# Dilated attention: value projections of 384 columns over a pair's three groups, and four weight units a pair

## The reference

```python
def mixer_dilated(x, w_in, w_out, table):
    proj = x @ w_in                       # [256, 1024] @ [1024, 3 * 3 * 1024]
    gw = 3 * ATTN_WIDTH
    for g, (window, dilation) in enumerate(DILATED_PAIRS):
        q, k, v = [split_heads(t, N_HEADS) for t in jnp.split(proj[..., g * gw:(g + 1) * gw], 3, axis=-1)]
        o, lse = dilated_group(q, k, v, table, window, dilation)
        outs.append(o); lses.append(lse)
    wts = jax.nn.softmax(jnp.stack(lses), axis=0)
    o = jnp.einsum('gbhs,gbhsd->bhsd', wts, jnp.stack(outs).astype(jnp.float32))
    return merge_heads(o.astype(x.dtype)) @ w_out
```

## Time and profile before

| what | value |
|---|---|
| median of 3 runs | 2671.15 us (2669.37 to 2674.56) |
| profiled execution | 2666.07 us, span of its instructions 2664.1 us, mean granted TensorE clock 0.962 |
| busy over the span | PE 2478.7 us (93%), weight loads 2106.7 us (79%), DVE 1533.5 us (58%), ACT 1098.9 us (41%), POOL 20.5 us (1%) |
| 896 products of 256 columns, high x high, in the page | 292 ns each, 261.6 us |
| 608 products of 512 columns, high x high, feed-forward | 393 ns each, 239.1 us |
| 24 loads of dilated weights | 1536 KB each, 6.7 us from issue to landing (median) |

### The profile page before, as it was taken

How to read it: one execution, slowest core, us unless ns; L and a number is a source line. 1 busy time by engine, 2 the same in 40 slices (tenths; PEclk the granted TensorE clock), 3 DMA queues, 4 the chain that set the end, 5 groups by cost and what they waited for, 6 DMA issues and landing times.

```text
span 2664.1 us, 37436 instructions
## 1 busy us (share of the span) xinstructions
PE 2478.7 (93%) x15464; PEld 2106.7 (79%) x15464; DVE 1533.5 (58%) x2133; ACT 1098.9 (41%) x1150; POOL 20.5 (1%) x35
## 2 busy tenths in 40 slices
PE   7999999999999799998999978889999999896997
PEld 6999986888879578886887956768878888484886
DVE  3334334666668646667666456466656654754565
ACT  3333332455446425554554322145545533312553
POOL 1000000000000000000000000000000000000000
PEclk9999988999999879999999989989999999999999
DMA  5333323355522315554454411025535543100453
GB/s 206 113 137 107 133 111 111 135 187 185 186 112 96 134 57 189 188 186 170 151 186 183 158 48 71 2 98 187 188 140 189 189 159 141 60 12 33 144 187 110
DMA packets 35712, 358.29 MB, mean 134 GB/s; under 512 B 4111, under 2 KB 4255, under 8 KB 6544
## 3 DMA queue, kind: packets, MB, share of 16 engines
q1 hardware_dynamic: 32512, 342.39, 35.3%
q0 software_dynamic: 3104, 14.51, 1.7%
HBM read 355.76 MB, written 1.12 MB: 134 GB/s over the span
## 4 chain that ended last, share of the span: by engine, by line
PE 83%; DVE 9%; ACT 4%; DVEq 2%; issue 1%; DMA 1%; ACTq 0%; SPq 0%
PE psum L663 21%; PE psum L412 12%; PE psum L413 11%; PE psum L414 11%; PE psum L665 10%; PE psum L614 2%; PE psum L1800 2%; DVE ring_lo L426 1%; PE psum L943 1%; PE psum L1811 1%; PE psum L921 1%; PE psum L1807 1%; ACT ring_hi L420 1%; PE psum L788 1%; PE psum L552 1%
## 5 line engine op out<-in xcount | busy, mean ns | idle before, releaser
L663 PE MATMUL psum<-xT_both,ring_hi 128*128 128x512 f32 x2432 | 874.4, 402 | 2.3 <-DVE ring_lo L426 2.2
L426 DVE TENSOR_TENSOR ring_lo<-ring,ring_hi 128x3072 fp32r<-128x3072 f32 (+1 forms) x188 | 622.7, 3312 | 245.7 <-ACT ring_hi L420 245.7
L665 PE MATMUL psum<-xT_both,ring_lo 128*128 128x256 f32 x2432 | 685.7, 282 | 0.0
L663 PEld LDWEIGHTS psum<-xT_both,ring_hi 128*128 128x128 f32 x2432 | 461.4, 190 | 119.0 <-DVE ring_lo L426 4.8
L420 ACT CAST ring_hi<-ring 128x3072 fp32r<-128x3072 f32 (+1 forms) x188 | 511.1, 2719 | 43.7 <-DMA ring<-moe_w 29.6
L665 PEld LDWEIGHTS psum<-xT_both,ring_lo 128*128 128x128 f32 x2432 | 463.3, 190 | 5.8
L706 ACT COPY scratch<-psum 128x512 f32<-128x512 f32 x152 | 89.4, 588 | 607.2 <-PE psum L665 607.2
L412 PE MATMUL psum<-xT_both,ring_hi 128*128 128x256 f32 x896 | 261.6, 292 | 23.6 <-DVE ring_lo L1027 11.0
L413 PE MATMUL psum<-xT_both,ring_hi 128*128 128x256 f32 x896 | 256.6, 286 | 0.0
L414 PE MATMUL psum<-xT_both,ring_lo 128*128 128x256 f32 x896 | 256.3, 286 | 0.0
L412 PE MATMUL psum<-ring_hi,glu_hi 128*128 128x512 f32 x608 | 239.1, 393 | 3.2 <-DVE glu_lo L743 3.2
(11 more groups left out here) (356 smaller groups left out, 3257.8 us busy)
## 6 DMA issues: line engine op xcount, KB each, us to landing
ring<-ff_w SPq DMA_DIRECT2D x88, 1536.0 KB, 6.6
ring<-moe_w SPq DMA_DIRECT2D x64, 1536.0 KB, 6.6
ring<-dil_w SPq DMA_DIRECT2D x24, 1536.0 KB, 6.7
ring<-mix_w SPq DMA_DIRECT2D x20, 1536.0 KB, 6.7
ring<-proj_w SPq DMA_DIRECT2D x16, 1024.0 KB, 4.8
ring<-sb_w SPq DMA_DIRECT2D x8, 1536.0 KB, 6.7
scratch<-rel_dram POOLq DMA_DIRECT2D x16, 384.0 KB, 4.4
rowv<-row_vectors POOLq DMA_DIRECT2D x4, 1024.0 KB, 5.0
```

The source lines that it names most:

```text
L426: nc.vector.tensor_tensor(ring_lo[:, s, 0:floats], ring[:, s, 0:floats], ring_hi[:, s, 0:floats].bitcast(F32), ALU.subtract).then_inc(low_ ...
L663: nc.tensor.matmul(psum[:, bank, :].rearrange("p (w n) -> p w n", w=2), ring_hi[:, s, cols], xT_both[:, :, k, :], start=(k == 0), stop=False)
L665: last = nc.tensor.matmul(psum[:, bank, 0:SEQ], ring_lo[:, s, cols], xT_hi[:, k, :], start=False, stop=(k == KC - 1))
```

## The change

The weights of the dilated stage are laid out anew: per pair three units with Q and K of one group (2048 floats a partition, 1 MB) and one unit with V of all three groups (3072 floats, 1.5 MB), in slots 0 to 2 and 3. `ring_hi` gets a second view, `dil_hi`, in which the four units stand one behind the other. `project_v(p, t)` now makes one tile of tokens for all three groups at once: 24 products of 384 moving columns, twice a pair, and `take_v` copies 384 columns. SP loads in the order 0, V, 1, 2, and asks for a slot again when PE has read it (`qk_ready`, `v_ready`), not when the copy is done. PE's order in a pair becomes scores 0, 1, QK 0, turn 0, scores 2, V of tile 0, weigh 0, turn 1, V of tile 1, scores 3, weigh 1, turn 2, QK 1, weigh 2, turn 3, QK 2, weigh 3. The lists of DVE and ACT, and what all three do ahead of the loop, are changed with it. The counts of `high_ready` and `low_ready` go up by four a pair.

```diff
     out = {"x": f["x"][0], "rel_table": f["rel_table"], "router_b": f["router_b"],
            "router_w": rows(f["router_w"]), "positions": f["positions_2"].astype(np.int32)}
     w = f["dil_w_in"][0].reshape(KC, P, GROUPS, 3, PAIRS, P)
-    out["dil_w"] = w.transpose(4, 2, 1, 0, 3, 5).reshape(PAIRS, GROUPS, P, UNIT)
+    out["dil_qk"] = w[:, :, :, 0:2].transpose(4, 2, 1, 0, 3, 5).reshape(PAIRS, GROUPS, P, 2 * D)
+    out["dil_v"] = w[:, :, :, 2].transpose(3, 1, 0, 2, 4).reshape(PAIRS, P, UNIT)
     w = f["sb_w_in"][0].reshape(KC, P, 3, PAIRS, P)
     out["sb_w"] = w.transpose(3, 1, 0, 2, 4).reshape(PAIRS, P, UNIT)
     mixers = [0, 1, 4, 5, 6, 7, 2, 3]
...
                 r.count[s] += 1
             r.next = (first + n) % SLOTS
+        DIL_V = GROUPS
+
         def load_dilated(sp):
-            for g in range(GROUPS):
-                sp.dma_start(ring[:, g, :], d["dil_w"][0, g]).then_inc(ring_full[g], 16)
+            for u in (0, DIL_V, 1, 2):
+                src = d["dil_v"][0] if u == DIL_V else d["dil_qk"][0, u]
+                sp.dma_start(ring[:, u, 0:unit_floats(u)], src).then_inc(ring_full[u], 16)
             with sp.Fori(1, PAIRS) as p:
-                for g in range(GROUPS):
-                    sp.wait_ge(v_copied, p * GROUPS + (g + 1 - GROUPS))
-                    src = d["dil_w"].rearrange("a g p n -> (a g) p n")[bass.ds(p * GROUPS + g, 1)]
-                    sp.dma_start(ring[:, g, :], src.rearrange("o p n -> (o p) n")).then_inc(ring_full[g], 16)
-            sync_ring.skip(range(GROUPS), PAIRS)
+                for u in (0, DIL_V, 1, 2):
+                    if u == DIL_V:
+                        sp.wait_ge(v_ready, p * TILES)
+                        src = d["dil_v"][bass.ds(p, 1)]
+                    else:
+                        sp.wait_ge(qk_ready, p * GROUPS + (u + 1 - GROUPS))
+                        src = d["dil_qk"].rearrange("a g p n -> (a g) p n")[bass.ds(p * GROUPS + u, 1)]
+                    sp.dma_start(ring[:, u, 0:unit_floats(u)], src.rearrange("o p n -> (o p) n"))\
+                      .then_inc(ring_full[u], 16)
+            sync_ring.skip(range(SLOTS), PAIRS)
             sp.dma_start(tab[:, P:], d["tables"][:, P:]).then_inc(tables_loaded, 16)
-            for g in range(GROUPS):
-                sync_ring.silent[g] = PAIRS
-            sp.wait_ge(v_copied, PAIRS * GROUPS)
+            for u in range(SLOTS):
+                sync_ring.silent[u] = PAIRS
+            sp.wait_ge(v_ready, PAIRS * TILES)
+            sp.wait_ge(qk_ready, PAIRS * GROUPS)
+
+        def unit_floats(u):
+            return UNIT if u == DIL_V else 2 * D
+
+        def unit_hi(u):
+            return dil_hi[:, u * 2 * D:u * 2 * D + unit_floats(u)]
+
+        def unit_turn(u):
+
+            return (0, 2, 3, 1)[u]
         sync_ring, pe_ring, act_ring, dve_ring = Ring(), Ring(), Ring(), Ring()
...
             pe = nc.tensor
-            def project_qk(p, g, par, turn):
-                pe.wait_ge(low_ready, 3 * p + (3 * turn + g + 1))
+            def project_qk(p, g):
+                pe.wait_ge(low_ready, SLOTS * p + (unit_turn(g) + 1))
                 if not (isinstance(p, int) and p == 0 and g == 0):
                     pe.wait_ge(qk_copied, 3 * p + g)
                 for part in range(2):
                     for k in range(KC):
-                        cols = slice(k * 384 + part * P, k * 384 + (part + 1) * P)
-                        last = products(psum[:, 0, part * SEQ:(part + 1) * SEQ], ring_hi[:, g, cols],
+                        cols = slice(k * SEQ + part * P, k * SEQ + (part + 1) * P)
+                        last = products(psum[:, 0, part * SEQ:(part + 1) * SEQ], unit_hi(g)[:, cols],
                                         ring_lo[:, g, cols], xT_hi[:, k, :], xT_lo[:, k, :],
                                         start=(k == 0), stop=(k == KC - 1))
                 last.then_inc(qk_ready, 1)
-            def project_v(p, g, par):
-                if not (isinstance(p, int) and p == 0 and g == 0):
-                    pe.wait_ge(v_copied, 3 * p + g)
-                for t in range(TILES):
-                    for k in range(KC):
-                        tok, cols = slice(t * P, (t + 1) * P), slice(k * 384 + 2 * P, k * 384 + 3 * P)
-                        last = products(psum[:, 1, tok], xT_hi[:, k, tok], xT_lo[:, k, tok],
-                                        ring_hi[:, g, cols], ring_lo[:, g, cols],
-                                        start=(k == 0), stop=(k == KC - 1))
+            def project_v(p, t):
+
+                if t == 0:
+                    pe.wait_ge(low_ready, SLOTS * p + (unit_turn(DIL_V) + 1))
+                if not (isinstance(p, int) and p == 0 and t == 0):
+                    pe.wait_ge(v_copied, TILES * p + t)
+                for k in range(KC):
+                    tok, cols = slice(t * P, (t + 1) * P), slice(k * GROUPS * P, (k + 1) * GROUPS * P)
+                    last = products(psum[:, 1, 0:GROUPS * P], xT_hi[:, k, tok], xT_lo[:, k, tok],
+                                    unit_hi(DIL_V)[:, cols], ring_lo[:, DIL_V, cols],
+                                    start=(k == 0), stop=(k == KC - 1))
                 last.then_inc(v_ready, 1)
...
-                qk = lambda g: more and project_qk(p + 1, g, 1 - par, 0)
-                vv = lambda g: more and project_v(p + 1, g, 1 - par)
+                qk = lambda g: more and project_qk(p + 1, g)
+                vv = lambda t: more and project_v(p + 1, t)
                 scores(p, 0, par); scores(p, 1, par); qk(0)
                 turn_probs(p, 0, par); scores(p, 2, par); vv(0)
-                weigh(p, 0, par); turn_probs(p, 1, par); qk(1)
-                scores(p, 3, par); weigh(p, 1, par); turn_probs(p, 2, par); vv(1)
-                weigh(p, 2, par); qk(2)
-                turn_probs(p, 3, par); vv(2); weigh(p, 3, par)
+                weigh(p, 0, par); turn_probs(p, 1, par); vv(1)
+                scores(p, 3, par); weigh(p, 1, par); turn_probs(p, 2, par); qk(1)
+                weigh(p, 2, par); turn_probs(p, 3, par); qk(2); weigh(p, 3, par)
             pe.wait_ge(turned_used, pe_u.turned)
-            for g in range(GROUPS):
-                project_qk(0, g, 0, 0)
-                project_v(0, g, 0)
-                if g == 0:
-                    pe_rel_bias()
+            project_qk(0, 0)
+            pe_rel_bias()
+            project_v(0, 0)
+            project_v(0, 1)
+            project_qk(0, 1)
+            project_qk(0, 2)
             pe.wait_ge(rel_copied, 1)
             body(0, 0, True)
             body(1, 1, True)
...
                 body(i * 2 + 1, 1, True)
             body(PAIRS - 2, 0, True)
             body(PAIRS - 1, 1, False)
...
-            def take_v(p, g, par):
-                v.wait_ge(v_ready, 3 * p + g + 1)
-                v.tensor_copy(v_sb[:, par, g, :], psum[:, 1, 0:SEQ]).then_inc(v_copied, 1)
+            def take_v(p, t, par):
+                v.wait_ge(v_ready, TILES * p + t + 1)
+                v.tensor_copy(v_sb[:, par, :, t * P:(t + 1) * P],
+                              psum[:, 1, 0:GROUPS * P].rearrange("p (g n) -> p g n", g=GROUPS)).then_inc(v_copied, 1)
...
-            def split(p, g):
-                v.wait_ge(high_ready, 3 * p + (g + 1))
-                v.tensor_tensor(ring_lo[:, g, :], ring[:, g, :], ring_hi[:, g, :].bitcast(F32), ALU.subtract)\
+            def split(p, u):
+                n = unit_floats(u)
+                v.wait_ge(high_ready, SLOTS * p + (unit_turn(u) + 1))
+                v.tensor_tensor(ring_lo[:, u, 0:n], ring[:, u, 0:n], unit_hi(u).bitcast(F32), ALU.subtract)\
                  .then_inc(low_ready, 1)
             def body(p, par, more, more2):
-                vv = lambda g: more and take_v(p + 1, g, 1 - par)
+                vv = lambda t: more and take_v(p + 1, t, 1 - par)
                 biased_max(p, 0, par); biased_max(p, 1, par)
                 normalise(p, 0, par); normalise(p, 1, par); more and split(p + 1, 1)
-                biased_max(p, 2, par); vv(0); normalise(p, 2, par); more and split(p + 1, 2)
-                biased_max(p, 3, par); vv(1); normalise(p, 3, par); more2 and split(p + 2, 0); vv(2)
+                biased_max(p, 2, par); vv(0); normalise(p, 2, par); vv(1)
+                biased_max(p, 3, par); normalise(p, 3, par); more and split(p + 1, 2)
+                if more2:
+                    split(p + 2, 0)
+                    split(p + 2, DIL_V)
...
             split(0, 0)
-            split(0, 1)
             v.wait_ge(rel_ready, 1)
             v.tensor_copy(rel_rows[0:HEADS, :].rearrange("p (g n) -> p g n", g=GROUPS),
                           psum[0:HEADS, 4:7, 0:3 * P]).then_inc(rel_copied, 1)
+            split(0, DIL_V)
+            split(0, 1)
+            take_v(0, 0, 0)
             split(0, 2)
-            for g in range(GROUPS):
-                take_v(0, g, 0)
+            take_v(0, 1, 0)
             split(1, 0)
...
-            def split(p, g):
```

(63 more changed lines are left out.)

## The result

The changed kernel takes 2603.4 us (median of 4 runs, 2600.1 to 2605.1) against 2670.3 us (4 runs, 2663.6 to 2674.6): ratio 0.9752, 95% interval 0.9739 to 0.9764. Direction and mechanism were right; the gain was 67 us (68 from the first median of before, 2671.2) where 58 were forecast. Its profiled execution took 2603.6 us, 62.5 less than that of before.

The account below looks back on a forecast made before the run. TensorE's own instructions were taken to bound the dilated stage. Seven pairs at 7.8 us less (54.6) plus 3.2 at the start gave 57.8 us: 2666.1 to 2608.3 profiled, plus 5.1 makes 2613 us, range 2604 to 2627.

Parts of the forecast that it names:

- The value products: Steady pair: 48 products of 384 columns at 0.1745 us replace 144 at 0.113 us, 7.8 us less a pair.
- rival B: Value products: 384 columns cost like 512 (0.229 us, kernel 2634 us) or like 256 (0.120 us, 2592 us); 5% together.
- No new stall in the steady pair: Pairs projecting for the next: loads, splits and copies stay covered, so a pair takes 37.2 us.
- the prediction's walk: Steady pair's new order timed from s, the end of the pair before; weigh 3 ends at s + 37.3.
- Covers of 0.4 and 0.6 us: Steady pair: work hiding copies, 0.4 us to spare for qk(2), 0.6 us for qk(1) and tile 0.
- rival A: Joints of a steady pair: covers fail slightly or the clock falls, 0.5 to 1.9 us a pair, 2617 to 2627 us; 15%.
- Rival C: Steady pair: loads or splits set it, freed time is idle, pair over 40 us, kernel 2632 us or more; 3%.
- Rival D: ScalarE's in-order wait for V: each microsecond of landing over 12.5 us lengthens the pair by one; slower from 20.3 us; 1%.
- The start: Ahead of and into pair 1: smaller first load, 4.8 us TensorE wait for V's split, 1.5 us half clock; gain 3.2 us.
- Only moved earlier: Pair 7 and everything behind it: starts earlier but gains no time of its own.
- the shift by 5.1 us: Whole kernel: the profiled execution lay 5.1 us below the median of three runs, so 5.1 us was added to the forecast.
- The chances: Whole kernel: forecast 76%, small stalls 15%, product width 5%, idle freed time 3%, same 1%, slower 2%.

Follow-up runs that it names:

- The late load: Changed kernel with SP's loop order 0, 1, V, 2 in place of 0, V, 1, 2, so V is asked for behind unit 1; 2665.9 us (one run).
- v_width_128: Changed kernel with each value product of 384 columns cut into three of 128; 2678.0 us (7 runs), ratio to before 1.0044.

## Why the prediction was right, and where it was off

- **The value products.** Forecast 0.1745 us, measured 0.177; 7.8 us a pair, measured 7.6. Reading the cost of a product from the distance of starts, not from the durations in a row, and laying 384 on the line of 256 and 512 was right. Neither end of rival B came.
- **No new stall in the steady pair.** 37.42 us for 37.2; of the 0.2 us the width is 48 x 0.003 = 0.1. In the prediction's walk the last steps don't add up (qk(2) to s + 36.5 and 1.45 us of weigh 3 make s + 38, not 37.3); in the trace weigh 3 starts at s + 36.0. Covers of 0.4 and 0.6 us held; rival A did not come. Rival C neither.
- **Rival D's limit.** I put V's slack at 12.5 us of landing, 6 above its 6.6. The late load shows the same wait and chain at about the place worked out. The price was too low: by rival D's rule, each microsecond beyond the slack is one of the pair, 9 us later would have cost 3 us, and it cost 10.5, of which 5.7 are clock, which the rule left out.
- **The start.** 3.2 us plus pair 0's 7.8 were forecast, 11.0 measured (104.77 - 93.77), by errors that cancel: V's products started at 31.2, not 30.45, since the bias products ended later than I had them; and at 57.9 us the clock did not fall, as I had assumed because it had at the earlier trace rows; that saved about 1.2 us (57.9 to 63.9 for 57.2 to 64.4), and the turn then waited 0.28 us for VectorE. That the two numbers agree to 0.1 us is luck.
- **Pair 7 and behind.** "Only moved earlier" was off by 5.5 us in the profiled pair of executions: 2.7 in pair 7 and 2.8 behind it. Of the 2.7, 2.1 are gone when the second trace of before is taken (19.1 us). Of the 2.8, 2.2 lie ahead of the norm of the first layer: in the first trace of before the output projection began at half clock (0.63 us a product for 0.39). Its second trace doesn't have them. The norm's first row, in the first and second trace of before and in that of after, comes 27.3, 25.1 and 25.1 us behind the copy that ends pair 7:

```profile
423.53 1.88 DVE L467 BATCH_NORM_STATS2 stat<-x_rows 128x6 f32<-128x512 f32 x3
```

```profile
419.90 1.28 DVE L467 BATCH_NORM_STATS2 stat<-x_rows 128x6 f32<-128x512 f32 x2
```

```profile
361.94 1.29 DVE L488 BATCH_NORM_STATS2 stat<-x_rows 128x6 f32<-128x512 f32 x2
```

That second trace of before lost time further on instead. From the copy that ends pair 6 to the end of the span the two traces of before have 2289.1 and 2286.2 us, those of after 2283.6 and 2281.6, and the eight others lie between 2281.1 and 2287.3. So by the traces taken the two kernels differ there by 2.6 to 7.5 us, and a part of that is scatter between executions. How much of it is the change's stays open.
- **The term that missed most** is the shift by 5.1 us from the profiled execution to the median. Both traces of before come from executions below its medians (2666.1 and 2663.4, medians 2669 to 2671), while the changed kernel's median lies near its profiled executions (2603.4 and 2603.6; 2603.6 and 2601.8). 57.8 forecast, 1.1 less in the stage, 5.5 in and behind pair 7, 5.6 of shift and what lies around the span make the 67.8 us between the medians. Where the slower executions of before lose their 5 us no trace shows; that stays open. The stage itself gave 56.7 us for 57.8; the other 11 us of the gain are nothing that the prediction worked out, and they put the median at the edge of the range.
- **The chances** add up to 102%: forecast, A, B and C have 99, and 1% same and 2% slower come on top.

## What to carry to other kernels

Measure a product by the distance between starts, at several widths: when narrower ones cost the same, join operands that share a stationary tile until it is the columns that are paid. Before doing so, walk each engine's list for the load behind which other work stands: here one place later in a list cost as much as the wide product gave. Idle stretches of TensorE can cost twice, by themselves and by the clock behind them (here 4.7 us of wait and 5.7 of half clock a pair), so have the next operands split before they are due.

## What the runs showed that I had not expected

- The floor goes with the clock. Four products of `v_width_128` on both sides of the change from 128 to 256 columns, at half clock:

```profile
60.17 0.41 PE L434 MATMUL psum<-ring_lo,xT_both 128*128 128x128 f32 x1
...
62.30 0.41 PE L435 MATMUL psum<-dil_hi,xT_both 128*128 128x128 f32 x1
...
62.84 0.41 PE L434 MATMUL psum<-xT_both,dil_hi 128*128 128x256 f32 x1
...
64.55 0.41 PE L433 MATMUL psum<-xT_both,dil_hi 128*128 128x256 f32 x1
```

128 columns go 2.13 / 10 = 0.213 us apart, 256 columns 1.71 / 8 = 0.214; at full clock 0.113 and 0.120. So the floor nearly doubles when the clock halves: it is 256 cycles at 1.2 GHz and 271 at 2.4 GHz, not a fixed time. The Trainium skill (TensorE: Matmul & The Clock Gate, LDWEIGHTS) gives the weight load by the columns of the weights at 1.2 GHz, 107 ns for 128, with no other value for the lower clock; that fits the 0.113 and not the 0.213, so here the measurement decides.
- In the same kernel TensorE was busy for 30.5 of 31.2 us in products of 128 columns at a granted clock of 0.50, and the clock rose 2.4 us after the first product of 256 columns, at 64.9.
